# Projecting the index queries of a sparse-attention layer for fewer token columns

## What is computed

```
u = hn @ w_in
xa, za, q, k, v, zb, iq, ik, iw = jnp.split(u, IN_OFFSETS, axis=-1)
...
adm = (key_pos[None, :] // CHUNK) <= (q_pos[:, None] // CHUNK)
s = jnp.einsum('bthd,bsd->bths', iq, ik_all)
score = jnp.einsum('bths,bth->bts', jax.nn.relu(s), iw)
score = jnp.where(adm[None], score, neg)
_, idx = lax.top_k(score, topk)
```

## Time and profile before

| | us |
|---|---|
| median of 3 runs | 1140.67 |
| the runs | 1139.57 to 1142.98 |
| span of the profiled execution, first to last instruction | 1138.8 |
| PE busy (share of the span) | 1045.8 (92%) |
| DVE busy | 867.4 (76%) |
| ACT busy | 495.6 (44%) |
| POOL busy | 391.9 (34%) |

### The profile page before, as it was taken

One profiled execution on the slowest core, in us unless ns is written; L12 is line 12 of the kernel. 1 busy time (PEld: TensorE's weight loads), 2 busy tenths in 40 slices (PEclk: granted clock), 3 DMA queues, 4 the chain that ended last, 5 costly groups with the idle time before them and its releaser, 6 DMA issues.

```text
span 1138.8 us, 16568 instructions
## 1 busy us (share of the span) xinstructions
PE 1045.8 (92%) x5914; PEld 937.4 (82%) x5914; DVE 867.4 (76%) x1643; ACT 495.6 (44%) x827; POOL 391.9 (34%) x247
## 2 busy tenths in 40 slices
PE   5989897999989998989999996899999899999996
PEld 3689765899989998989899996778888778888873
DVE  1667799999998899999999996667667656444344
ACT  4332365312223667655576234556665534111111
POOL 0222465411212255545446572233331242122120
PEclk9989999999999998999999998999999999999998
DMA  9612001222323122222123621334312336242221
GB/s 299 186 42 66 19 1 39 67 86 76 117 77 99 42 79 79 79 61 60 38 79 96 210 80 61 99 85 120 93 48 75 93 93 213 58 126 94 83 66 55
DMA packets 128280, 100.78 MB, mean 88 GB/s; under 512 B 12176, under 2 KB 119200, under 8 KB 128224
## 3 DMA queue, kind: packets, MB, share of 16 engines
q1 hardware_dynamic: 128224, 100.04, 29.8%
HBM read 74.04 MB, written 25.99 MB: 88 GB/s over the span
## 4 chain that ended last, share of the span: by engine, by line
PE 56%; DVE 24%; issue 13%; ACT 4%; DMA 1%; SPq 1%; POOL 1%; DVEq 0%; ACTq 0%
PE ps L554 16%; PE ps L555 15%; PE ps L556 15%; DVE scores L1982 6%; PE ps L1702 5%; DVE best L1978 4%; DVE y_a L2031 3%; DVE hidden L2026 2%; DVE conv L2004 2%; PE ps L1437 2%; DVE scores L1942 1%; PE ps L1422 1%; DVE mult L2021 1%; DVE mult L2012 1%; PE ps L1532 1%
## 5 line engine op out<-in xcount | busy, mean ns | idle before, releaser
L554 PE MATMUL ps<-h_hi,w_hi 128*128 128x364 f32 (+1 forms) x984 | 326.3, 332 | 4.8 <-DVE h_lo L1880 4.1
L555 PE MATMUL ps<-h_lo,w_hi 128*128 128x364 f32 (+1 forms) x984 | 325.3, 331 | 0.0
L556 PE MATMUL ps<-h_hi,w_lo 128*128 128x364 f32 (+1 forms) x984 | 325.0, 330 | 0.0
L876 POOL TENSOR_TENSOR w_lo<-w_raw,w_hi 128x1024 fp32r<-128x1024 f32 (+1 forms) x41 | 106.2, 2591 | 327.8 <-ACT w_hi L1067 327.8
L554 PEld LDWEIGHTS ps<-h_hi,w_hi 128*128 128x128 f32 (+1 forms) x984 | 185.3, 188 | 6.5 <-issue 4.2
L555 PEld LDWEIGHTS ps<-h_lo,w_hi 128*128 128x128 f32 (+1 forms) x984 | 185.3, 188 | 1.4
L556 PEld LDWEIGHTS ps<-h_hi,w_lo 128*128 128x128 f32 (+1 forms) x984 | 185.2, 188 | 0.7
L1982 DVE MATCH_REPLACE8 scores<-best,scores 128x512 f32<-128x512 f32 (+6 forms) x204 | 172.3, 855 | 0.0
L1978 DVE MAX8 best<-scores 128x8 f32<-128x512 f32 (+6 forms) x204 | 162.8, 859 | 2.1 <-DVE scores L1925 0.2
L1082 ACT ACTIVATE stage<-ps 128x364 f32<-128x364 f32 (+1 forms) x66 | 29.6, 474 | 140.1 <-PE ps L556 131.8
L986 POOL TENSOR_TENSOR y_lo<-y_raw,y_hi 128x1024 fp32r<-128x1024 f32 (+1 forms) x18 | 41.3, 2296 | 142.2 <-ACT y_hi L1339 142.2
(11 more groups left out here) (246 smaller groups left out, 2121.2 us busy)
## 6 DMA issues: line engine op xcount, KB each, us to landing
w_raw<-in_w_in SPq DMA_DIRECT2D x40, 512.0 KB, 4.7
w_mod_raw<-in_w_mod SPq DMA_DIRECT2D x8, 1024.0 KB, 12.3
y_raw<-y_scratch SPq DMA_DIRECT2D x16, 512.0 KB, 4.3
wo_raw<-in_w_out SPq DMA_DIRECT2D x10, 512.0 KB, 5.0
q_scratch<-stage SPq DMA_DIRECT2D x8, 546.0 KB, 3.6
y_scratch<-y_a SPq DMA_DIRECT2D x8, 546.0 KB, 3.6
zb_scratch<-stage SPq DMA_DIRECT2D x8, 546.0 KB, 4.2
x_in<-in_x_prompt SPq DMA_DIRECT2D x8, 512.0 KB, 8.3
```

Source lines behind the costliest of these rows:

```text
L554: nc.tensor.matmul(out, w_part_hi, x_hi, start=first, stop=False)
L555: nc.tensor.matmul(out, w_part_hi, x_lo, start=False, stop=False)
L556: return nc.tensor.matmul(out, w_part_lo, x_hi, start=False, stop=last)
L876: pool.tensor_tensor(w_lo[:, slot, :, 0:width], w_raw[:, slot, :, 0:width], f32(w_hi[:, slot, :, 0:width]), ALU.subtract).then_inc(w_lo_do ...
```

## The change

The four sets of index queries are computed for the token columns 256 to 1091 only. Their three chunks are 280, 278 and 278 columns wide instead of 364; set 0, the index keys, and all other sets keep 364. ACT's reads of these four sets into `stage` and DVE's copies and subtractions into `iq_parts` run over the same 836 columns. Columns 0 to 255 of `iq_parts` are no longer written. The number of instructions on each engine, their order and their waits stay as they are.

```
--- before.py
+++ after.py
@@ -46,6 +46,7 @@
 SM_SCALE = P ** -0.5
 IW_SCALE = (NH * IDX) ** -0.5
 NT = 9
+INDEX_FIRST = 2 * P
 ROUND_ONE_TILES = (7, 6, 5, 4, 3, 2)
 
 
@@ -63,6 +64,17 @@
 
 S_LRU, S_ZB = 17, 49
 SETS_PER_STEP = 4
+
+
+def all_cols(c):
+
+    return slice(CH * c, CH * (c + 1))
+
+
+def index_cols(c):
+
+    cut = [INDEX_FIRST, INDEX_FIRST + 280, INDEX_FIRST + 558, TP]
+    return slice(cut[c], cut[c + 1])
 
 
 def tile_at(i):
@@ -1072,16 +1084,17 @@
                 act.wait_ge(h_full, 2 * k + 2)
                 nc.scalar.activation(h_hi[:, k, :], x_t[:, k, :], ACT.Copy).then_inc(h_hi_done, 1)
 
-            def read_set(s, dst, func, m=P, bias=None):
+            def read_set(s, dst, func, m=P, bias=None, cols=all_cols):
 
                 for c in range(NCH):
                     act.wait_ge(set_ready, s * 3 + (c + 1))
                     b = 3 * (read_set.parity) + c
-                    d = dst[0:m, CH * c:CH * (c + 1)]
+                    d = dst[0:m, cols(c)]
+                    src = ps[0:m, b, 0:cols(c).stop - cols(c).start]
                     if bias is None:
-                        x = nc.scalar.activation(d, ps[0:m, b, 0:CH], func)
+                        x = nc.scalar.activation(d, src, func)
                     else:
-                        x = nc.scalar.activation(d, ps[0:m, b, 0:CH], func, bias=bias)
+                        x = nc.scalar.activation(d, src, func, bias=bias)
                     x.then_inc(set_read, 1)
                 read_set.parity = 1 - read_set.parity
             read_set.parity = 0
@@ -1102,7 +1115,7 @@
                     act.wait_ge(ik_parts, 12)
                 if m >= 2:
                     act.wait_ge(iq_done, 4 * (m - 1))
-                read_set(j, stage[:, j % 2, :], ACT.Copy)
+                read_set(j, stage[:, j % 2, :], ACT.Copy, cols=index_cols)
                 split_w(j % 2, (j + 2) // 2 + 1, 3 * j + 3)
 
             for u, (i, h, p_) in enumerate(INDEX_UNITS):
@@ -1466,16 +1479,16 @@
                 x = nc.tensor.transpose(ps[:, 0, 2 * m:2 * m + 2], mod_rows[0:2, P * m:P * (m + 1)], ident[0:2, 0:2])
             x.then_inc(mod_ready, 1)
 
-            def project(j, s, slot, width=P, first=False):
+            def project(j, s, slot, width=P, first=False, chunk=all_cols):
 
                 pe.wait_ge(w_lo_done, j + 1)
                 for c in range(NCH):
 
                     if not first:
                         pe.wait_ge(set_read, s * 3 + (c + 1 - 6))
-                    out = ps[0:width, 3 * project.parity + c, 0:CH]
+                    cols = chunk(c)
+                    out = ps[0:width, 3 * project.parity + c, 0:cols.stop - cols.start]
                     for k in range(KT):
-                        cols = slice(CH * c, CH * (c + 1))
                         x = split3(k, w_hi[:, slot, k, 0:width], w_lo[:, slot, k, 0:width],
                                    h_hi[:, k, cols], h_lo[:, k, cols], out, k == 0, k == KT - 1)
                     x.then_inc(set_ready, 1)
@@ -1493,9 +1506,9 @@
                 for j in range(2):
                     width = (72, P)[j]
                     for c in range(NCH):
-                        cols = slice(CH * c, CH * (c + 1))
+                        cols = (all_cols, index_cols)[j](c)
                         x = split3(k, w_hi[:, j, k, 0:width], w_lo[:, j, k, 0:width], h_hi[:, k, cols], h_lo[:, k, cols],
-                                   ps[0:width, 3 * j + c, 0:CH], k == 0, k == KT - 1)
+                                   ps[0:width, 3 * j + c, 0:cols.stop - cols.start], k == 0, k == KT - 1)
                         if k == KT - 1:
                             x.then_inc(set_ready, 1)
 
@@ -1516,7 +1529,7 @@
                     x.then_inc(ik_t, 1)
             for m in range(1, 4):
                 j = J_IQ + m
-                project(j, j, j % 2)
+                project(j, j, j % 2, chunk=index_cols)
 
             pe.wait_ge(ik_parts, 12)
             pe.wait_ge(ik_read, 2)
@@ -1909,15 +1922,14 @@
             lower, upper = slice(0, IDX), slice(IDX, P)
             for m in range(4):
                 j = J_IQ + m
-                src = stage[:, j % 2, :]
+                src = stage[:, j % 2, INDEX_FIRST:]
+                even, odd = iq_parts[:, 2 * m, INDEX_FIRST:], iq_parts[:, 2 * m + 1, INDEX_FIRST:]
                 dve.wait_ge(set_read, 3 * j + 3)
-                V.tensor_copy(iq_parts[lower, 2 * m, :], src[lower]).then_inc(iq_done, 1)
-                V.tensor_copy(iq_parts[upper, 2 * m + 1, :], src[upper]).then_inc(iq_done, 1)
+                V.tensor_copy(even[lower], src[lower]).then_inc(iq_done, 1)
+                V.tensor_copy(odd[upper], src[upper]).then_inc(iq_done, 1)
                 dve.wait_ge(iq_done, 4 * m + 2)
-                V.tensor_tensor(iq_parts[upper, 2 * m, :], src[lower], f32(iq_parts[lower, 2 * m, :]),
-                                ALU.subtract).then_inc(iq_done, 1)
-                V.tensor_tensor(iq_parts[lower, 2 * m + 1, :], src[upper], f32(iq_parts[upper, 2 * m + 1, :]),
-                                ALU.subtract).then_inc(iq_done, 1)
+                V.tensor_tensor(even[upper], src[lower], f32(even[lower]), ALU.subtract).then_inc(iq_done, 1)
+                V.tensor_tensor(odd[lower], src[upper], f32(odd[upper]), ALU.subtract).then_inc(iq_done, 1)
 
             def mask(i):
```

## The result

The changed kernel takes 1131.62 us in the median of 6 runs, the kernel before 1140.53 in the median of 6 in the same rounds. One of the six changed runs, at 1698.11 us with a granted clock of 0.55, was in a slower state and is left out of every comparison; the other five go from 1128.4 to 1135.43 with a median of 1130.15. The ratio is 0.9916, with a 95% interval from 0.99 to 0.9933: 9.6 us less (7.6 to 11.4). Two later sets of rounds of the same kernel gave 0.9875 (0.9857 to 0.9892) and 0.9909 (0.9888 to 0.9929). The mean of the three is 0.990, 11.4 us. These ratios are not the quotients of the medians, which differ by 10.4, 12.4 and 11.4 us in the three sets, also 11.4 in the mean. The forecast was 1129.4, from 1126.3 to 1133.0.

A forecast was written before the change was run, and what follows sets the result against it. PE was taken to lead (busy 92%), with PE and DVE both full after the index scores; 2.35 + 8.2 + 0.8 = 11.35, say 11.3 us, off the 1138.8 us span, plus 1.9 us, gave 1129.4 us, range 1126.3 to 1133.0.

The forecast's parts named there:

- What a narrower matmul costs: PE's index-query matmuls: about 128 ns at 278.7 columns instead of 166.2 at 364, from a line between 256 and 364.
- step 2: Sets two to four on PE: 216 matmuls x 38 ns saved, 8.2 us, if PE is never kept waiting.
- Step 1: First set, in the loop over k with the index keys: a lead of 2.35 us at the keys' end.
- rival A: Keys' end: DVE's cast takes the port before POOL's w_lo, set two up to 0.7 us later; 1130.1 us, chance 0.18.
- Rival B: Index-query projections: DVE becomes the bound, scores start late, priced at 3 us; 1132.4 us, chance 0.09.
- Step 3: Tail from set four's last matmul to DVE's first score: 0.8 us less through narrower reads, casts and subtractions.
- Step 4: After the first score: nothing is altered, so the gain moves the rest and costs nothing.

The follow-up runs named there:

- first set only: Against the kernel before: DVE's splits cut to 836 columns and only the first set narrow on PE and ACT, other three sets at 364; 1138.82 us, ratio 0.9977.

## Why the prediction was right

**What a narrower matmul costs** held: 128 ns expected, 128.2 measured, and for the last three sets 8.2 us (27.9 against 36.05, where the clock stays up), as in step 2. The line between 256 and 364 columns was right because 256 lies already on the slope; the floor it was to be set against is 112 ns and reaches up to about 240 columns. That 256 lay on the slope the prediction could only suppose from one width (118 ns, 5 above its 113).

**Step 1** was right for the clock that it supposed. I gave 2.35 us, on the clock rising at the same time as before, and at equal time at 1.2 GHz the traces give 2.3 (first set only against the first trace before). In the first trace after, set two starts 3.6 us sooner behind the loop's start; 1.2 of them come from 2.7 us of the loop at 1.2 GHz instead of 5.3. That stretch of 6.8 us began at 56.2 us (58.5 before), ahead of the loop's first narrow matmul, so it isn't the change's doing, and the second trace before, with 3.3 us of it, is at 28.0 us. Against the mean of the two traces before, 28.5, the three after, 25.5 in the mean, give 3.0 us. The order of POOL and DVE at the keys' end, rival A, had a margin of 0.09 us by my sum and 0.10 us in the trace. That was more than luck: the margin is 0.43 us in the four traces with a wide first set and 0.08 to 0.10 in the nine with narrow chunks of 278 or 418 columns, always with POOL ahead. The Trainium skill's rule for the shared pair (SBUF — State Buffer, Who interferes with whom) is that the one that issues first keeps the pair for its whole instruction, when DVE runs in a mode that uses both ports. The trace agrees: POOL issued first, and a cast of 0.69 us took 2.79.

**Step 2** was right as a term and then lost 1.5 us to a clock fall in all three traces of the changed kernel: 29.4 for 27.9. I had looked at the clock for what it did in each stretch of before and priced no fall that was not there. Rival B had no part in it: DVE stood idle 3.84 us before the fourth set's splits, and no set waited for weights. **Step 3**, 0.8 us expected, is 0.9 (7.7 to 6.8), and the kernel with narrow splits alone shows it by itself. The sum of the three was 11.35; at equal clock the traces give 2.3 + 8.2 + 0.9 = 11.4. As they ran, from mean to mean, 72.2 to 61.7, they give 10.5 us, which is 1.5 less for the fall in b and 0.6 more for the clock in a. The measured times give 11.4 us as the mean of the three ratios.

**Step 4**, that nothing later takes it back, holds in d, f and h. In the pair of traces that I compared first it seemed not to hold, because e was 1.5 us longer after. The second trace of before settles that this is a clock fall that both kernels can have; whether both have it equally often is open, as said above.

The first measurement, 9.6 us by the ratio (10.4 by the medians), lies below the sum; the second, about 14 us (12.4 by the medians), above. That the mean of three lands on the sum to 0.1 us is luck: the sixteen undisturbed runs of the changed kernel lie between 1125.5 and 1135.4 us. The traces show that executions differ by clock falls, in a, d, e, f and g, and by the 3.2 us ahead of a; that these make up the difference between the sets of rounds is argued, since only the profiled execution of each has a trace.

## What to carry to other kernels

A matmul's price by width has a floor and a slope, and both can be read from distances between starts in the kernel's own trace before a column is cut; cut down to the floor and no further, since chunks of 140 and 240 columns cost the same. Compare a stage at equal time at the lower clock before its size is called wrong: stage a differed by 3.6 us between two traces, and 1.2 of them were the clock's. Compare two kernels stage by stage between landmarks, with two traces of each at least: the part that was changed repeats within 1 us, while stages that nobody touched differ by 1.5 to 8 us, as far as the traces show through the clock. An edit that prevents a clock fall in one stage has earned nothing until the median over several runs says so.

## What the runs showed that I had not expected

- At 2.4 GHz a column above the floor costs 0.443 ns, not 1/2.4 = 0.417; at 1.2 GHz the distance is 233 ns for 280 columns, 0.83 ns a column, just 1/1.2.
- 140 and 240 columns cost the same 112 ns, each with its own weight load of 128 columns, and the same 213 ns at 1.2 GHz. With weights of 64 columns 64 columns cost 56 ns.
- TensorE's clock fell behind stretches in which PE had little to do, at places that differ between executions of the same kernel: at 341 us in one trace of before, not in the other; behind set two in three traces of the changed kernel, not in one with the same instructions there. Each of these stretches of 3.4 us cost 1.5 us.
- Attention, g, took from 286.0 to 294.1 us in fourteen traces without an edit in it, with 9.0 us at 1.2 GHz in the shortest and 25.0 in the longest; it makes the largest part of the difference between these traces, before the 3.2 us ahead of the loop over k and single falls in d, e and f.
